# The chunk inversion merged on VectorE, head 0 loaded ahead of it, and the exponents' sums moved to GpSimd

## The reference, cut to what matters

```
g = jnp.cumsum(chunks(g), axis=-1)
decay = jnp.exp(jnp.where(incl, g[..., :, None] - g[..., None, :], -jnp.inf))
lower = jnp.where(strict, jnp.einsum('nbhid,nbhjd->nbhij', k_beta, k) * decay, 0.0)
sol = lax.linalg.triangular_solve(eye + lower, rhs, left_side=True, lower=True)
a_qk = jnp.einsum('nbhid,nbhjd->nbhij', q, k) * decay
```

## Time and profile before

| What | Value |
|---|---|
| runs of the kernel before | 3602.71, 3599.6, 3594.38 us; median 3599.6 |
| span of the profiled execution | 3593.9 us (5.7 us under the median; no device time of its own is listed for it) |
| TensorE, VectorE, ScalarE, GpSimd busy | 82%, 68%, 39%, 12% of the span |
| preparation and inversion | from about 766 to 879 us |
| first stages of the core | from 879 to 942 us |
| steps of the heads | from 942 to about 1300 us |

### The profile page before, as it was taken

One profiled execution on the slowest core, in us unless ns is written; L12 is line 12 of the kernel. 1 busy time (PEld: TensorE's weight loads), 2 busy tenths in 40 slices (PEclk: granted clock), 3 DMA queues, 4 the chain that ended last, 5 costly groups with the idle time before them and its releaser, 6 DMA issues.

```text
span 3593.9 us, 39044 instructions
## 1 busy us (share of the span) xinstructions
PE 2958.7 (82%) x13702; PEld 2438.5 (68%) x13702; DVE 2447.2 (68%) x2263; ACT 1405.9 (39%) x1379; POOL 416.3 (12%) x371
## 2 busy tenths in 40 slices
PE   1699999950677769899999999776628799999998
PEld 1577787740466658678888888655527588888886
DVE  7488888847577734577878777578885655555555
ACT  0267543320355543433333333444434433333333
POOL 0001002324233300000000000023340000000000
PEclk6699999975799879999999999888768899999999
DMA  9466677941544535488888888332214566566663
GB/s 364 173 218 238 237 249 290 377 149 50 93 95 94 83 107 191 164 310 308 319 338 307 320 328 329 117 124 97 93 47 141 189 207 213 198 211 204 204 210 129
DMA packets 337018, 729.19 MB, mean 203 GB/s; under 512 B 48961, under 2 KB 81809, under 8 KB 311089
## 3 DMA queue, kind: packets, MB, share of 16 engines
q1 hardware_dynamic: 331584, 708.67, 57.8%
q0 software_dynamic: 5360, 19.57, 1.6%
HBM read 708.49 MB, written 19.69 MB: 203 GB/s over the span
## 4 chain that ended last, share of the span: by engine, by line
PE 65%; DVE 18%; issue 6%; DMA 5%; ACT 4%; DVEq 1%; SPq 0%; POOL 0%; ACTq 0%; POOLq 0%
PE psg L628 19%; PE psg L630 19%; PE psg L629 19%; DVE y L1445 5%; DVE wlo L1002 2%; DMA aring<-in_ada_w 2%; DMA wraw<-in_gdn_in_w 2%; PE psn L650 1%; PE pst L784 1%; DVE wraw L1307 1%; ACT dec L1715 1%; PE pst L616 1%; DVE cv L1128 1%; DVE sinv L379 1%; DVE stmp L374 1%
## 5 line engine op out<-in xcount | busy, mean ns | idle before, releaser
L1002 DVE TENSOR_TENSOR wlo<-wraw,whi 128x2048 fp32r<-128x2048 f32 x441 | 1017.5, 2308 | 604.1 <-ACT whi L1528 602.3
L1528 ACT ACTIVATE whi<-wraw 128x2048 fp32r<-128x2048 f32 x441 | 844.6, 1916 | 1390.4 <-PE psg L630 1280.0
L628 PE MATMUL psg<-whi,h_hi 128*128 128x512 f32 (+1 forms) x2592 | 1043.5, 403 | 152.7 <-DVE wlo L1002 135.6
L629 PE MATMUL psg<-wlo,h_hi 128*128 128x512 f32 (+1 forms) x2592 | 1026.7, 396 | 0.0
L630 PE MATMUL psg<-whi,h_lo 128*128 128x512 f32 (+1 forms) x2592 | 1026.5, 396 | 0.0
L628 PEld LDWEIGHTS psg<-whi,h_hi 128*128 128x128 f32 x2592 | 502.5, 194 | 274.4 <-DVE wlo L1002 135.7
L630 PEld LDWEIGHTS psg<-whi,h_lo 128*128 128x128 f32 x2592 | 501.3, 193 | 105.7
L629 PEld LDWEIGHTS psg<-wlo,h_hi 128*128 128x128 f32 x2592 | 502.7, 194 | 102.1 <-issue 1.9
L1012 DVE SCALAR_TENSOR_TENSOR aacc<-aring,cond,aacc 128x2048 f32<-128x2048 f32 x153 | 366.0, 2392 | 2.0 <-DMA aring<-in_ada_w 1.7
L628 PE MATMUL psg<-whi,g_hi 128*128 128x512 f32 x704 | 279.7, 397 | 0.4 <-DVE wlo L1002 0.4
L629 PE MATMUL psg<-wlo,g_hi 128*128 128x512 f32 x704 | 276.0, 392 | 0.0
(11 more groups left out here) (213 smaller groups left out, 2830.3 us busy)
## 6 DMA issues: line engine op xcount, KB each, us to landing
aring<-in_ada_w SPq DMA_DIRECT2D x192, 1024.0 KB, 7.0
wraw<-in_ffn_in_w SPq DMA_DIRECT2D x176, 1024.0 KB, 5.8
wraw<-in_gdn_in_w SPq DMA_DIRECT2D x97, 1024.0 KB, 5.2
wraw<-in_ffn_out_w SPq DMA_DIRECT2D x88, 1024.0 KB, 5.2
wraw<-in_cf_pw_w SPq DMA_DIRECT2D x48, 1024.0 KB, 5.1
wraw<-in_gdn_out_w SPq DMA_DIRECT2D x32, 1024.0 KB, 5.0
rr<-d_rows SPq DMA_DIRECT2D x16, 1024.0 KB, 15.0
d_qkn<-kn POOLq DMA_DIRECT2D x8, 512.0 KB, 3.5
```

Source lines behind the costliest of these rows:

```text
L628: mm(o, ah, wh, start=first and j == 0, stop=False)
L629: mm(o, ah, wl, start=False, stop=False)
L1002: tt(wlo[:, j % 2, :], wraw[:, j % 4, :], whi[:, j % 2, :].bitcast(F32), SUB).then_inc(w_lo, 1)
L1528: av(whi[:, j % 2, :], wraw[:, j % 4, :], ACT.Copy).then_inc(w_hi, 1)
```

## The change

- `invert` takes all four channels in one product and one sum a step, on VectorE alone. To make the directions alike, direction 1's blocks are built transposed (the broadcasts of L1219 are swapped for it), and `sinv` gets eight slots: 2 to 5 are worked on, two copies fill 6, 7 and 0, 1 with transposes. GpSimd no longer takes part.
- The memory is laid out anew, so that what head 0 needs doesn't lie on what the inversion uses. `exb` gets a place of its own; `rr` moves to slot 2 and `inv` to slot 3 of `wraw`.
- SP stores `rows` a second time as `d_rr` (eight DMAs of 16 partitions), a head's eight rows in one piece of 8 KB. It loads `qk` and `rr` of head 0, then `qk` of head 1 and `vt` of head 0, and only then waits for the inversion. `d_inv` is stored in two parts: partitions 0 to 15 (heads 0 and 1), whose landing `load_inv(0)` waits for, and the rest.
- VectorE makes head 0's masks before the inversion.
- The twelve sums of `exb` go to GpSimd, behind `rv` and ahead of part C; head 0's come before the inversion's end. GpSimd's steps are written out one by one. `t64` is summed in two instructions.

```diff
+        def invert(count):
+            work = sinv[:, 2:6]
+            for j in range(31):
+                n, m = 31 - j, j + 1
+                shape = [P, 4, n, m]
+                tmp = stmp[:, :, 0:n * m].rearrange("p c (i k) -> p c i k", k=m)
+                to = work[:, :, m:32, 0:m]
+                count.wait(nc.vector)
+                count.inc(nc.vector.tensor_tensor(tmp, sdec[:, :, m:32, j].unsqueeze(3).broadcast_to(shape),
+                                                  work[:, :, j, 0:m].unsqueeze(2).broadcast_to(shape), MUL))
+                count.wait(nc.vector)
+                count.inc(nc.vector.tensor_tensor(to, to, tmp, ADD))
+            count.wait(nc.vector)
+            for to, of in ((6, 2), (0, 4)):
+                count.inc(nc.vector.tensor_copy(sinv[:, to:to + 2].rearrange("p c i j -> p c j i"), sinv[:, of:of + 2]))
...
+        rr = wraw[:, 2, :].rearrange("p (c t) -> p c t", t=T)
+        inv = wraw[:, 3, :].rearrange("p (s t m) -> p s t m", s=8, t=TT)
...
             sp.dma_start(srow[:, :, :], d_rows.rearrange("(c h) (b i) -> (h b) c i", h=HQ, i=32)).then_inc(s_land, 16)
-            sp.wait_ge(c_v, C_INV)
-            sp.wait_ge(c_init, C_POOL_INV)
-            sp.dma_start(d_inv.rearrange("p a c i j -> p (a c i j)"),
-                         sinv[:, :, :, :, :].rearrange("p a c i j -> p (a c i j)")).then_inc(inv_out, 16)
-            sp.wait_ge(inv_out, 16)
-            sp.wait_ge(c_init, C_POOL_INV + 1)
...
-                sp.dma_start(rr[:, :, :], d_rows.rearrange("(c h) t -> h c t", h=HQ)[ds(h, 1)].rearrange(
-                    "a c t -> (a c) t").partition_broadcast(P)).then_inc(rr_land, 16)
+                sp.dma_start(rr[:, :, :].rearrange('p c t -> p (c t)'), d_rr[ds(h, 1)].rearrange("a c t -> (a c t)").partition_broadcast(P)).then_inc(rr_land, 16)
...
+            for c in range(8):
+                sp.dma_start(d_rr[:, c, :], rows[HQ * c:HQ * (c + 1), :]).then_inc(rr_out, 16)
+            load_qk(0)
+            sp.wait_ge(rr_out, 16 * 8)
             load_rr(0)
-            load_qk(0)
-            core_loads(-1, z=False)
+            sp.wait_ge(kq_done, 1)
+            load_qk(1)
+            load_v(0)
+            sp.wait_ge(c_v, C_INV)
+            d_flat, s_flat = d_inv.rearrange("p s i j -> p (s i j)"), sinv[:, :, :, :].rearrange("p s i j -> p (s i j)")
+            sp.dma_start(d_flat[0:16], s_flat[0:16]).then_inc(inv_out0, 16)
+            sp.dma_start(d_flat[16:P], s_flat[16:P]).then_inc(inv_out, 16)
+            sp.wait_ge(c_init, C_POOL + 2)
+            sp.wait_ge(inv_out0, 16)
+            load_inv(0)
+            sp.wait_ge(ex_done, 1)
+            load_rr(1)
+            sp.wait_ge(inv_out, 16)
             core_loads(0, z=False)
...
-                if M:
-
-                    dve.wait_ge(rr_land, 16 * (h + 2))
-                    dve.wait_ge(d1_done, h + 1)
-                    for c in range(4):
-                        for seg, t, kind, tj in ((0, 0, 0, 0), (2, 1, 0, 1), (1, 1 - c // 2, 1, c // 2)):
-                            i = ts(exb[:, c, :, seg, :], rr[:, 2 * c:2 * c + 2, t * P:(t + 1) * P],
-                                   ncum[:, kind, tj, c, ds(h + 1, 1)], 0.0, ADD, MIN)
-                    i.then_inc(ex_done, 1)
             step(-1, 1, A=False, B=False, C=False)
+            invert(pr)
+            assert pr.n == C_INV
+            pr.wait(dve)
             step(0, 0, B=False, C=False)
...
+                if M:
+                    pool.wait_ge(rr_land, 16 * (h + 2))
+                    if h >= 0:
+                        pool.wait_ge(ex_done, h + 1)
+                        pool.wait_ge(d1_done, h + 1)
+                    for c in range(4):
+                        for seg, t, of, tj in ((0, 0, 0, 0), (2, 1, 0, 1), (1, 1 - c // 2, 1, c // 2)):
+                            i = nc.gpsimd.tensor_scalar(exb[:, c, :, seg, :], rr[:, 2 * c:2 * c + 2, t * P:(t + 1) * P],
+                                                        ncum[:, of, tj, c, h + 1:h + 2], 0.0, ADD, MIN)
+                    i.then_inc(ex_done, 1)
                 if C:
                     pool.wait_ge(on_done, h - 1)
...
+            pool.wait_ge(c_v, C_ROWT)
+            step(-1, 1, A=False, C=False)
+            pool.wait_ge(c_v, C_INV)
             step(0, 0, C=False)
             step(1, 1, C=False)
-            with pool.Fori(1, HQ // 2) as i:
-                for s in range(2):
-                    step(2 * i + s, s)
+            for h in range(2, HQ - 2):
+                step(h, h % 2)
```

More of the change, by code:

```diff
@@ L165, in build @@
         ada_st.close()
[L167 to L174, removed]
         epoch = ExitStack()
+        sinv = sb("sinv", [P, 8, 32, 32], at=epoch)
+        sdec = sb("sdec", [P, 4, 32, 32], at=epoch)
+        skk = sb("skk", [P, 32, 32], at=epoch)
+        tri = sb("tri", [P, 4, P], at=epoch)
         ba2 = sb("ba2", [P, TT, P], at=epoch)
@@ L207, in build @@
         oms = sb("oms", [P, 3, 4], at=p2a)
+        rv = sb("rv", [P, 2, 2, 4, P], at=p2a)
+        sb("apart", [P, 896], at=p2a)
+        ncum = sb("ncum", [P, 2, TT, 4, HQ], at=p2a)
+        beta = sb("beta", [P, TT, 4, HQ], at=p2a)
+        masks = sb("masks", [P, 2, 2, 3, P], at=p2a)
+        m64 = sb("m64", [P, 2, P], at=p2a)
+        exb = sb("exb", [P, 4, 2, 3, P], at=p2a)
+        qk = sb("qk", [P, 2, T], at=p2a)
+        vt = sb("vt", [P, TT, 2, P], at=p2a)
+        yh = sb("yh", [P, 4, P], at=p2a)
+        mk = sb("mk", [P, 2, 2, 3, P], at=p2a)
+        dec = sb("dec", [P, 2, 4, 2, 3, P], at=p2a)
+        free_slot = wraw[:, (G_GO + 3) % 4, :].rearrange("p (a b c m) -> p a b c m", a=2, b=4, c=TT)
+        wt = free_slot[:, 0]
+        assert (G_GO + 1) % 4 == 2 and (G_GO + 3) % 4 == 0
+        uu = free_slot[:, 1].rearrange("p b c m -> p (b c m)").rearrange("p (o c m) -> p o c m", o=2, c=4)
+        rr = wraw[:, 2, :].rearrange("p (c t) -> p c t", t=T)
+        inv = wraw[:, 3, :].rearrange("p (s t m) -> p s t m", s=8, t=TT)
         p2a.close()
@@ L353, in build @@
         C_G, C_ROWT, C_ROWS, C_SUB, C_DEC = 5, 13, 14, 17, 21
-        C_INV = C_DEC + 2 * (2 * 31 + 1)
+        C_INV = C_DEC + 2 * 31 + 2
         C_POOL = 22
-        C_POOL_INV = C_POOL + 2 * 31 + 1
         block = stack.enter_context(nc.Block())
[L360 to L379, removed]
-            count.wait(engine)
-            for _, c, *_ in steps:
-                count.inc(ops.tensor_copy(sinv[:, 1, c].rearrange("p c i j -> p c j i"), sinv[:, 0, c]))
@@ L804, in w_stage @@
                         for t in range(TT):
[L805 removed]
+                            i = mm(ps_w[:, 2 * c + t, :], lm[:, c, t, :], inv[:, slot_of(0, c), t, :], start=True, stop=True)
                     i.then_inc(w_done, 1)
@@ L1294, in step @@
                     dve.wait_ge(t_done, 2 * h + 2)
-                    tt(t64[:, par].rearrange("p c t m -> p (c t) m"), ps_w,
-                       inv[:, 1].rearrange("p c t m -> p (c t) m"), ADD).then_inc(t64_done, 1)
+                    for d in range(2):
+                        s = slot_of(1, 2 * d)
+                        i = tt(t64[:, par, 2 * d:2 * d + 2].rearrange("p c t m -> p (c t) m"), ps_w[:, 4 * d:4 * d + 4],
+                               inv[:, s:s + 2].rearrange("p c t m -> p (c t) m"), ADD)
+                    i.then_inc(t64_done, 1)
                 if C:
```

70 lines of the change are left out of this document (27 added, 43 removed).

## The result

| | before | after |
|---|---|---|
| median of the runs | 3598.6 us (16 runs, 3591.1 to 3607.6) | 3609.9 us (16 runs, 3605.8 to 3624.3) |
| profiled execution: span | 3593.9 | 3604.5 (its device time 3606.0) |
| first h stage | 942.38 | 911.62 |
| the fourteen steps together; one of them | 309.9; 22.1 | 354.3; 25.3 |
| from the last h stage to SP's load of the output weights (1300.92, 1312.19) | 48.6 | 46.3 |

What follows compares the result with a forecast made beforehand. The inversion, then a string of transfers, then a ring of dependences with ScalarE's wait for VectorE's sums bound the kernel. First heads 39.8 + fourteen steps 31.9 = 71.7 us gained: 3599.6 - 71.7 = 3528 us, range 3508 to 3553.

Steps and rivals of the forecast that it cites:

- The price of a sum: Twelve `exb` sums on GpSimd: 0.45 us each for 256 elements, 5.4 us together, ends 3.8 and 9.3.
- X: Time of a head's twelve `exb` sums on GpSimd, taken as 5.4 us, ends 3.8 and 9.3.
- Collision of head 0's sums with the inversion: Head 0's sums on GpSimd meet `sdec`'s products or the inversion's first steps: 4 us taken.
- The inversion: On VectorE alone it takes 60.9 us against 72.1 before, ending at 874.5, 5 us earlier.
- The first heads: From the inversion to the first h stage: 902.6 instead of 942.4, gain 39.8 us, ends some 32 and 47.
- its rival: `rr` in one piece still lands in 15 us instead of 5.4: total gain 40, 3559 us; chance 0.08.
- The fourteen steps: Steps from the first h stage: 13 x 2.36 + 1.2 = 31.9 us gained, a step of 19.8.
- the 2.36 us: Gain a step without VectorE's sums: `oT` starts at 1046.85 rather than 1049.21, held next by the transposes.
- X up to 8.5 costs nothing: In a step, GpSimd's twelve sums may take 8.5 us without delaying `oT`; 9.3 costs 0.8 a step.
- GpSimd becomes the ring: Rival: GpSimd's part A, the sums and ScalarE's work set the step; at 1.27 us a sum, 3640 us; chance 0.05.
- 11.2 + X: Period if GpSimd decides: part A 7.0, ScalarE's `decays(0)`, `oT`, `decays(1)` 4.2, and the twelve sums; exceeds 22.1 from 10.9.
- has the same room: In a step, GpSimd's `og` product behind the sums was given their room: 1.4 us, and 1.8 more until `oT` is delayed.

Runs made afterwards that it cites:

- kernel with six sums in the gap: Changed kernel with six sums back on VectorE ahead of `second_half(1)`, where it waits for TensorE, and the second store behind head 1's `rr`: 3519.4 us, ratio 0.9781.
- kernel with the loads behind: Changed kernel with all sums on VectorE, head 0's loads, masks and sums behind the inversion, and one 4 MB store: 3569.9 us, ratio 0.992.
- six and six: Changed kernel with six of the twelve sums back on VectorE, behind `og`: 3541.3 us, ratio 0.983.
- late store: Changed kernel with six sums back on VectorE behind `og`, plus the second `d_inv` store issued behind head 1's `rr`: 3540.5 us, ratio 0.9826.

## Why the prediction was wrong

**What bounds the kernel** was read rightly: the inversion, a string of transfers, then a ring of dependences with ScalarE's wait for the sums in it. The kernel with six sums in the gap has the step that the prediction gave (19.7 against 19.8), with the wait that it named next.

**The price of a sum is the step that failed.** X was taken at 5.4 us, with ends of 3.8 and 9.3, and is 13.4: over the upper end by 4.1. The working doubled the 0.25 of a selection because it too reads one tensor, and called a product of two tensors the dear end because it reads twice as much. The measured prices don't go by reads: copy 0.36, two tensors 0.69, one tensor with two scalars 1.12. The trace of before had no row of this form, and the range was closed at 0.772, called "the one GpSimd row of this size". It wasn't: the earlier trace rows show 0.93 us for 255 elements on GpSimd beside VectorE, and twelve of those are 11.2 us, already past the 10.9 at which the prediction's own ring begins. Both rows are forms with one operation; the sum has two.

The sentence on the Trainium skill (GPSIMD Engine Reference, section 4.1), that GpSimd is roughly at line rate with one input, falls here by measurement: twelve sums take 3.2 to 4.3 us on VectorE, 0.27 to 0.36 each, and 13.4 on GpSimd, 1.12 each. By it the price was to be near the low end, 3.8 us; the low end was the farther one.

**Collision of head 0's sums with the inversion**: 4 us taken, 1.3 measured. The sums ran from 800.05 to 818.56. The inversion's first seven additions took 0.55, 0.67, 0.68, 0.78, 0.88, 0.97 and 0.96 us, where in the kernel with the loads behind they took 0.38, 0.41, 0.52, 0.62, 0.72, 0.81 and 0.89: 1.1 us; the products between them took the same in both, and `sdec` 0.2 more. GpSimd paid the larger part, 18.5 us for 13.4. That in the steps, beside instructions with an operand in PSUM, the sums would meet nothing was right: 13.4 as with VectorE idle.

**The inversion**: 60.9 us taken, 62.7 measured; without GpSimd's sums beside it 61.7. The formula from two rows held for products twice as long as any among them: 1.22 us for 1020 elements. Its end: 874.5 forecast, 871.1 measured. Of these 3.4 us, 1.0 comes from ahead of the core, 0.3 from the masks (1.9 us instead of 2.2) and 2.7 from the collision, and the inversion itself took some 0.7 back.

**The first heads**: 39.8 us taken, 30.8 measured. From the end of the inversion on: the store of 16 partitions 7.1 us instead of 5 (inside its bounds), the eight issues 10.3 instead of 3.9, `rr` of head 1 issued at 888.6 instead of 883.7. The wait in the queue that the prediction put on `rr` was in truth on SP's issues ahead of it: when the big store is issued behind them they take 4.8. Together with the inversion's earlier end these errors cancel: `rr` was there at 894.04, forecast 893. That agreement is luck. The 9.0 us that are missing at the h stage are this 1.0 and the 8.0 of the sums, 13.4 instead of 5.4. `rr` itself lands in 4.9, forecast 5.4, and its rival falls. (Its working was wrong too: half of 6.5 us on top of a step of 19.8 is 23.0, not 21.4.)

For the first store the Trainium skill (SBUF — State Buffer, section "Door 1: The DMA port swizzle") has a reason for the dear half of the bounds: by its table the first 16 partitions reach 4 of 16 ports. The whole tile moved 4 MB in 11.1 us; an eighth of the data at a quarter of the rate is half of that, an estimated 5.6. The row says 7.1, and 6.4 where the 3.5 MB come later; the full rate would have given 1.4, and 512 KB from all 128 partitions land in 3.5 (`d_qkn<-kn`, on GpSimd's queue). So the trace is on the page's side, but no run took the same bytes from other sets of partitions on SP's queue.

**The fourteen steps**: 31.9 us of gain taken, 44.4 of loss measured. The removed wait, the 2.36 us, and the wait of `oT` behind it are borne out by the kernel with six sums in the gap, not by the changed one. "X up to 8.5 costs nothing" is borne out at 6.8, and not tried at 8.5. X at 13.4 is beyond it.

**The rival that came true** is "GpSimd becomes the ring", with a chance of 0.05. Its point, X = 13 or 1.08 us an instruction, lies where the measurement is (1.12, and 0.3% slower); its price, taken at 1.27, was 3640. Its formula was short: 11.2 + X gives 24.6 at 13.4, and the step is 25.3. Read from the rows above, the lap is part A 6.9, sums 13.4, `og` 1.3, transposes 1.1, `oT` 0.6, `decays(1)` 1.9, and 0.1 between them: 25.3. With nine sums (10.1) and transposes of 0.65 the same parts give 21.5, and 21.54 was measured. The prediction had `decays(0)` in the place of `og` and the transposes, and said of `og` that it "has the same room"; it hadn't, once the sums ahead of it were late, and the new wait `PE psn <- POOL og`, 73.6 us, is that.

**The chance** was thus the second failure. The forecast rested on a price for which the trace had no row, and the rival began at X = 10.9, 17% above the upper end of 9.3. With no row of the form (one tensor, pointer, two operations), 0.05 for a price past that point was too firm; the sign of the whole change hung on it, since twelve sums a head are multiplied by fourteen heads.

## What to carry to other kernels

An operation that moves to another engine has to be priced there in its own form (kinds of operands, number of operations); if no row has that form, the range stays open upwards, and the break-even price is the figure to work out first. A ring can be shortened by moving less: six sums of twelve, started beside the six that stay, took out the same wait that twelve had only handed on. And what is queued behind the moved work on its new engine (here `og`) inherits its lateness.

## What the hardware showed

- GpSimd's operation of a tensor with two scalars costs 1.12 us for 256 fp32 elements a partition, 3.3 ns an element from 128 to 512, with VectorE idle and in the steps alike; beside `sdec`, the masks and the inversion's first products and additions it cost 1.54 (18.51 / 12), while the additions took up to 0.26 us longer each and the products no longer.
- VectorE's sum of the same shape took 0.27 us in a run of twelve at the first heads (3.24 / 12) and 0.36 in a steady step (4.29 / 12, below, the kernel before), with no sum on GpSimd in either. Six of them beside GpSimd's six took 0.38 each (2.28 / 6), so GpSimd's sums add at most 0.02.

```profile
1043.22 4.29 DVE L1307 TENSOR_SCALAR wraw<-rr,ncum 128x256 f32<-128x256 f32 x12
```

- A row sent to all partitions lands in 4.9 us as one piece of 8 KB and in 15.2 as eight pieces of 1 KB, with the same 1 MB.
- With a store of 3.5 MB just ahead on the same queue, SP's next eight issues took 10.3 us instead of 4.8 (six and six, without and with the late store).
- A store from 16 partitions took 7.1 us for 512 KB, 74 GB/s, where the whole tile went at 378.
- Four transposes of 128x128 took 0.60 us at a granted clock of 1.00 and 1.11 at 0.50, after TensorE had stood 6.1 us.
